# Delta rule: the first product of each doubling level from 32 by 32 blocks on array tiles of 32 by 32

## The chip, the cores and the metric

The kernel runs on one core of a Trainium2 chip, in one launch. The metric is the device time of that launch in microseconds (us); three runs of the kernel before the change gave 3674.04 (median), 3671.25 and 3676.92.

## The reference

Three layers run over one sequence of T = 2048 tokens with 1024 features, all in float32: sliding-window attention, a gated recurrence, and a hybrid layer whose two halves are a gated linear attention (GLA) and an RWKV-7 delta rule with 8 heads of 64. The change lies in the delta rule. Cut to what is computed there:

```python
def step(S, inp):                       # S: (head, value dim 64, key dim 64)
    r_t, w_t, k_t, v_t, kk_t, a_t = inp
    sa = einsum('bhvk,bhk->bhv', S, -kk_t)
    S = S * w_t[:, :, None, :] + sa[..., None] * (kk_t * a_t)[:, :, None, :] + v_t[..., None] * k_t[:, :, None, :]
    y = einsum('bhvk,bhk->bhv', S, r_t)
    return S, y
_, y = lax.scan(step, S0, xs)           # over 2048 tokens
```

The kernel doesn't scan token by token. It takes chunks of 64 tokens, in which the steps amount to a unit triangular system of 64 by 64 for each head. The inverse of that matrix is built by doubling: from the inverses of the diagonal blocks of size h (2, 4, 8, 16, 32) come those of size 2h, with the block under the diagonal being a product of three blocks: inverse, part of the matrix, inverse.

## The kernel before

`build` calls the phases one after the other; `delta_rule(k, h_saved)` comes after attention and the recurrence, and before the gated linear attention. Everything named below is in it.

**Tiling.** The 2048 tokens are 4 groups of G = 512, the 8 heads are 4 pairs p. That makes 16 units u = (group, pair), and each unit has two halves s of 256 tokens, so SN = 32 steps s. One step holds 4 chunks of 64 tokens for 2 heads: in SBUF the 128 partitions are two chunks c = 0, 1 (64 rows each), and the free dimension holds head h, chunk pair j and 64 columns. `m5(s)` is the part of the system matrix, `xz5(s)` the inverse so far and its transpose (index 0 and 1).

**A doubling level.** `halve(l, s, ...)` on TensorE (L2562 to L2585) does level l = 1 to 5 with h = 2^l, in two parts with a `yield` between them. The first part, L2564 to L2570, is called a here (l3a is that of level 3): for each h, j and c one product of the stored matrix with the inverse, 64 by 64 by 64, into one PSUM bank: 8 products. Its rows are `half(c)` and its output partitions `half(1 - c)`, so the 8 use two of the four array tiles of 64 by 64, the two off the diagonal. The second part, L2577 to L2584, is called b: VectorE (L2990) has multiplied a's result by the 0/1 mask `low{l}` into `t1`, and b multiplies the inverse with it from both sides: 8 products at L2580 (levels 1 to 4 alone) and 8 at L2583, all four tiles of 64 by 64 at levels below 5. VectorE adds them to the inverse at L2994 and L2995. `row // (2h) == small // (2h)` in the mask means that at levels 1 to 4 (2h up to 32) only the two diagonal blocks of 32 by 32 of a's result are used, and at level 5 only the block under the diagonal.

A product of float32 operands is two pairs of instructions, each pair a weight load and a matmul on the same array tile. So 8 products are 16 matmul records.

**The order of the work.** `in_turn` (L2436) writes the order of every engine's instructions by hand. It runs i over SN + 4 rounds of ten turns; in each turn TensorE takes one piece of `solve(i - 3)`, one of `scores(i - 2)`, one of `carry(i - 4)`, and then a number of pieces of `front(i)`. Front is the input projection: `product` (L194 to L196), three matmuls of 128x512 with 128 by 128 weights a piece. So each turn is a short section of small products between two stretches of front. The ten turns' sections on TensorE, before the change:

- turn 0: `lk` (L2626), l3a, transposes of `scores` (L2595), the first carry product c0 (L2674)
- turn 1: l3b, `m` and `x` (L2603, L2612), c1
- turn 2: l4a, c2
- turn 3: l4b, l1a, c3
- turn 4: l5a, l1b, `y` (L2681)
- turn 5: l5b, l2a, the mean over a head (L2687)
- turn 6: `wu` (L2638), l2b, the variance (L2691)
- turns 7 and 8: `gu` and `ry` of `solve`

The products c0 to c3 carry the state from chunk to chunk, 2 products (4 records) each on the two diagonal tiles of 64 by 64; c(i) waits for VectorE's update of the state (a `stt`, recorded at L183) after c(i-1). VectorE's pieces follow the same order in each turn: solve, scores, carry, front.

Of the kernel before, what the change touches and what calls it, by code (L numbers as in the profile page):

```python
# [2334 lines left out]
def delta_rule(k, h_saved):  # L2335
# [8 lines left out]
    def room(words):  # L2344

        if k.used + words <= k.arena_words:
# [30 lines left out]
    groups = [(g, p) for g in range(NG) for p in range(4)]  # L2377
    UN, SN = len(groups), 2 * len(groups)
    half = lambda i: slice(64 * i, 64 * i + 64)
    cols_of = lambda g: slice(g * G, (g + 1) * G)  # L2380
    lo_of = lambda g, c: k.hT_cut[:, c, cols_of(g)]
    hi_of = lambda g, c: k.hT_cut[:, c, cols_of(g // 2 if g == 2 else 0)] if g else k.oT_cut[:, 4 + c // 2, T // 2 + c % 2 * G:T // 2 + (c % 2 + 1) * G]
# [2 lines left out]
    m5 = lambda s: m_at[s % 2].rearrange("p (h i j m t) -> p h i j m t", h=2, i=2, j=2, m=2)  # L2385
    xz5 = lambda s: xz_at[s % 2].rearrange("p (m h j t) -> p m h j t", m=2, h=2, j=2)
# [8 lines left out]
    blocks = [("w", g, None) if p is None else (kind, g, p) for g in range(NG)  # L2395
              for p, kind in [(None, "w")] + [(p, kind) for p in range(4) for kind in "krvz"]]
# [96 lines left out]
    def on_pe():  # L2493
        mm = pe.matmul
        k.settle(pe)

        def bank(from_ring, kind, n):
            b, before = from_ring.take(kind, n)
            if before is not None:
                pe.wait_ge(*taken(*before))  # L2500
            return b
# [60 lines left out]
        def halve(l, s, ring, steps, came, t1, vec):  # L2562
            b = bank(ring, f"l{l}a", s)
            b4 = b[:, 0:SW].rearrange("p (h j t) -> p h j t", h=2, j=2)  # L2564
            pe.wait_ge(*came)
            for h in range(2):
                for j in range(2):
                    for c in range(2):
                        ins = mm(b4[half(1 - c), h, j, :], m5(s)[half(c), h, 0, j, 0, :], xz5(s)[half(c), 0, h, j, :], start=True, stop=True)
            ins.then_inc(*steps.did(f"l{l}a"))  # L2570
            yield
            x4 = bank(ring, f"l{l}X", s)[:, 0:SW].rearrange("p (h j t) -> p h j t", h=2, j=2) if l < 5 else None
            z4 = bank(ring, f"l{l}Z", s)[:, 0:SW].rearrange("p (h j t) -> p h j t", h=2, j=2)
            pe.wait_ge(*vec.by(f"t{l}", s))
            for h in range(2):
                for j in range(2):
                    if l < 5:  # L2577
                        for c in range(2):
                            o = half(1 - c)
                            mm(x4[half(c), h, j, :], xz5(s)[o, 1, h, j, :], t1[o, h, j, :], start=True, stop=True)  # L2580
                    for c in range(2):
                        o = half(1 - c)
                        ins = mm(z4[o, h, j, :], t1[o, h, j, :], xz5(s)[o, 1, h, j, :], start=True, stop=True)  # L2583
            ins.then_inc(*steps.did(f"l{l}b"))  # L2584
            yield  # L2585

        def scores(s):
# [26 lines left out]
            yield  # L2614
            yield
            yield from halve(1, s, sb, Spe, Sv.by("xd", s), t14[0], Sv)
            yield from halve(2, s, sb, Spe, Sv.by("X1", s), t14[0], Sv)

        def solve(s):
# [3 lines left out]
            for j in range(2):  # L2623
                for h in range(2):
                    for c in range(2):
                        ins = mm(b4[half(1 - c), j, h, :], m[half(c), h, 1, j, 0, :], tm[half(c), 2, j, h, :], start=True, stop=True)  # L2626
            ins.then_inc(*Vpe.did("lk"))
            yield from halve(3, s, sb, Vpe, Sv.by("X2", s), t14[1], Vv)
            yield from halve(4, s, sb, Vpe, Vv.by("X3", s), t14[1], Vv)
            yield from halve(5, s, sb, Vpe, Vv.by("X4", s), t14[1], Vv)  # L2630
# [459 lines left out]
def build(nc, ins, out, x1, x2, h2, spans, at):  # L3090
    with ExitStack() as ctx:
        k = Core(nc, ctx, ins, spans, at)
        constants(k)
        x0 = ins["x"][0]
        h_saved = h2.rearrange("(c p) t -> p c t", p=P)
        attention(k)
        finish_layer(k, x0, x1, ins["attn_w_out"][0], ins["attn_b_out"][0], ins["post_norm_w"][0], "pre1", None, head=RecurrenceHead)
        recurrence(k)
        finish_layer(k, x1, x2, ins["rec_w_out"][0], None, ins["post_norm_w"][1], "norm2", None, h_saved)
        delta_rule(k, h_saved)  # L3100
        gla(k)
        finish_layer(k, x2, out, ins["w_out_2"][0], None, None, None, ins["final_norm_w_2"])
        for s in k.stores:
            k.sp.wait_ge(*s.end())
# [32 lines left out]
```

## Time and profile before

| | |
|---|---|
| median of 3 runs (lowest, highest) | 3674.04 us (3671.25, 3676.92) |
| the profiled execution | 3675.65 us, its span 3674.4 us |
| granted TensorE clock, mean | 0.984 |
| PE (TensorE matmul) busy | 3497.8 us, 95% |
| PEld (weight load) busy | 2820.5 us, 77% |
| DVE (VectorE) busy | 2057.0 us, 56% |
| ACT (ScalarE) busy | 1719.8 us, 47% |
| POOL (GpSimd) busy | 1346.6 us, 37% |

PE busy is the union of the matmul records' spans. Their ends are modelled and overlap the next records by far (a record of 64 columns lasts 218 ns), so the time that a group of matmuls takes is read from the starts, not from the durations: the last start of a group is its start plus the group's time less the duration of one record.

### The profile page before, as it was taken

What the parts mean: (1) busy time and instruction counts of PE and PEld (TensorE: products, weight loads), DVE (VectorE), ACT (ScalarE), POOL (GpSimd) and SP (SyncE); (2) the same over time, 40 slices, a digit from 0 to 9 for tenths busy, and PEclk for the clock granted to TensorE, in tenths of its full rate; (3) what the DMA queues carried; (4) which work ended last, traced back from release to release, by engine and by line L of the source; (5) the groups of instructions that cost most, each with busy time, mean ns of one, the idle gap of its engine ahead of it and who ended that gap; (6) DMA issues with size and microseconds to landing.
All of it is one profiled execution on the core that took longest, in us unless ns stands there. A gap on an engine that the chain in (4) does not pass through costs nothing. (4 is left out here: it accounts for less than half of the span.)

```text
span 3674.4 us, 83152 instructions
## 1 busy us (share of the span) xinstructions
PE 3497.8 (95%) x34784; PEld 2820.5 (77%) x34784; DVE 2057.0 (56%) x4664; ACT 1719.8 (47%) x3161; POOL 1346.6 (37%) x1681
## 2 busy tenths in 40 slices
PE   8999998899899999999998989999999997999999
PEld 7888785688788877888787867777777776788777
DVE  4566766755655657555555446666666665343422
ACT  3455555522555556555554344444444442444522
POOL 5333321132444554544543323222232220544332
PEclk9999999999999999999998999999999998999999
DMA  4322211232110111101112341111111113322322
GB/s 137 92 66 78 61 53 35 81 104 93 30 41 24 41 30 30 41 24 41 30 35 86 135 138 48 43 43 41 44 37 43 43 37 111 86 70 70 104 81 92
DMA packets 252243, 231.26 MB, mean 63 GB/s; under 512 B 9120, under 2 KB 223072, under 8 KB 251872
## 3 DMA queue, kind: packets, MB, share of 16 engines
q1 hardware_dynamic: 251872, 225.94, 20.2%
q8 instruction: 279, 4.57, 0.5%
q14 instruction: 92, 0.75, 0.1%
HBM read 192.35 MB, written 33.55 MB: 61 GB/s over the span
## 5 line engine op out<-in xcount | busy, mean ns | idle before, releaser
L195 PE MATMUL bank<-hT_cut,arena_cut 128*128 128x512 f32 x2048 | 803.8, 392 | 0.0
L188 ACT ACTIVATE arena<-bank 128x512 f32<-128x512 f32 (+1 forms) x584 | 315.9, 570 | 585.0 <-PE bank L196 295.3
L194 PE MATMUL bank<-hT_cut,arena_cut 128*128 128x512 f32 x1240 | 552.4, 445 | 0.0
L196 PE MATMUL bank<-hT_cut,arena_cut 128*128 128x512 f32 x1240 | 488.1, 394 | 0.0
L194 PE MATMUL bank<-arena_cut,hT_cut 128*128 128x512 f32 (+1 forms) x1280 | 458.2, 358 | 27.0 <-DVE arena_cut L1152 22.4
L188 ACT ACTIVATE arena<-arena 128x512 f32<-128x512 f32 (+3 forms) x674 | 350.0, 555 | 251.3 <-POOL arena L1600 191.8
L195 PE MATMUL bank<-arena_cut,hT_cut 128*128 128x512 f32 (+1 forms) x1280 | 448.5, 350 | 0.0
L195 PEld LDWEIGHTS bank<-hT_cut,arena_cut 128*128 128x128 f32 x2048 | 387.3, 189 | 78.5 <-issue 18.6
L189 ACT ACTIVATE arena<-arena 128x256 f32<-128x256 f32 (+2 forms) x336 | 210.3, 627 | 411.4 <-DVE arena L178 187.5
L2850 POOL TENSOR_TENSOR arena_cut<-arena,arena_cut 128x256 fp32r<-128x256 f32 x272 | 218.1, 833 | 409.0 <-ACT arena_cut L188 409.0
L715 POOL TENSOR_TENSOR arena_cut<-arena,arena_cut 128x256 fp32r<-128x256 f32 x288 | 216.2, 779 | 412.9 <-ACT arena_cut L188 412.8
L194 PE MATMUL bank<-oT_cut,arena_cut 128*128 128x512 f32 x808 | 349.5, 433 | 7.1 <-POOL arena_cut L2850 5.1
L188 ACT ACTIVATE arena_cut<-arena 128x1024 fp32r<-128x1024 f32 (+2 forms) x338 | 294.8, 888 | 53.6 <-DMA arena<-in_attn_w_in 34.7
L196 PE MATMUL bank<-oT_cut,arena_cut 128*128 128x512 f32 x808 | 318.9, 395 | 0.0
L196 PE MATMUL bank<-arena_cut,oT_cut 128*128 128x512 f32 x768 | 305.5, 398 | 0.0
L1591 POOL TENSOR_TENSOR arena_cut<-arena,arena_cut 128x256 fp32r<-128x256 f32 x248 | 197.5, 820 | 286.2 <-ACT arena_cut L188 286.2
L194 PEld LDWEIGHTS bank<-arena_cut,hT_cut 128*128 128x128 f32 x1280 | 242.2, 189 | 74.5 <-issue 31.9
L194 PEld LDWEIGHTS bank<-hT_cut,arena_cut 128*128 128x128 f32 x1240 | 233.0, 188 | 71.9 <-issue 22.0
L196 PEld LDWEIGHTS bank<-hT_cut,arena_cut 128*128 128x128 f32 x1240 | 232.8, 188 | 53.5
L195 PEld LDWEIGHTS bank<-arena_cut,hT_cut 128*128 128x128 f32 x1280 | 242.3, 189 | 35.4 <-issue 1.4
L196 PE MATMUL bank<-arena_cut,hT_cut 128*128 128x256 f32 x896 | 250.4, 280 | 0.0
L188 ACT ACTIVATE arena<-bank,arena 128x512 f32<-128x512 f32 (+1 forms) x176 | 90.0, 559 | 291.3 <-PE bank L196 260.5
(269 smaller groups left out, 7194.3 us busy)
## 6 DMA issues: line engine op xcount, KB each, us to landing
arena<-in_w_in SPq DMA_DIRECT2D x100, 512.0 KB, 3.8
arena<-in_attn_w_in SPq DMA_DIRECT2D x144, 256.0 KB, 2.8
arena<-in_rec_w_in SPq DMA_DIRECT2D x62, 512.0 KB, 4.1
x_after<-arena SPq DMA_DIRECT2D x32, 512.0 KB, 2.6
arena<-x_after SPq DMA_DIRECT2D x32, 512.0 KB, 4.1
arena<-in_x SPq DMA_DIRECT2D x16, 512.0 KB, 3.6
h_after<-hT SPq DMA_DIRECT2D x4, 2048.0 KB, 7.7
hT<-h_after SPq DMA_DIRECT2D x4, 2048.0 KB, 16.5
```

The source lines that it names most:

```text
L188: return e.activation(out, a, f, bias=bias, scale=scale)
L189: return e.activation(out, a, f, bias=bias, scale=scale, accum_out=accum)
L194: pe.matmul(out, a[0], b[0], start=start, stop=False)
L195: pe.matmul(out, a[0], b[1], start=False, stop=False)
L196: return pe.matmul(out, a[1], b[0], start=False, stop=stop)
L715: ins = pool.tensor_tensor(w_lo[n % WN][:, c, :], raw[n % WN][:, c, :], w_hi[n % WN][:, c, :], ALU.subtract)
L1591: ins = pool.tensor_tensor(w_lo[i][:, c, :], raw[i][:, c, :], w_hi[i][:, c, :], ALU.subtract)
L2850: ins = pool.tensor_tensor(w_lo[n % 3][:, c:c + 2, :], raw[n % 3][:, c:c + 2, :], w_hi[n % 3][:, c:c + 2, :], ALU.subtract)
```

## The change

The product a is cut into blocks of 32 by 32. At levels 1 to 4 each of the 8 products becomes two, for the two diagonal blocks (`blocks` = (0,0), (1,1)); at level 5 it becomes one, for the block under the diagonal ((0,1): rows 0 to 31 of the operands, output partitions of the lower half). Rows and outputs are at `quarter(...)`, so each product runs on an array tile of 32 by 32 with 32 moving columns. What of the bank isn't written any more is what the mask multiplies by zero. Nothing else changes: not the bank, the wait, the semaphore increment after the last product, the mask, nor the order of the turns.

```diff
+    quarter = lambda i: slice(32 * i, 32 * i + 32)
...
             b4 = b[:, 0:SW].rearrange("p (h j t) -> p h j t", h=2, j=2)
             pe.wait_ge(*came)
+            blocks = [(r, r) for r in range(2)] if l < 5 else [(0, 1)]
             for h in range(2):
                 for j in range(2):
-                    for c in range(2):
-                        ins = mm(b4[half(1 - c), h, j, :], m5(s)[half(c), h, 0, j, 0, :], xz5(s)[half(c), 0, h, j, :], start=True, stop=True)
+                    for r, to in blocks:
+                        for c in range(2):
+                            rows, own = quarter(2 * c + r), quarter(2 * (1 - c) + to)
+                            ins = mm(b4[own, h, j, quarter(r)], m5(s)[rows, h, 0, j, 0, quarter(to)], xz5(s)[rows, 0, h, j, quarter(r)],
+                                     start=True, stop=True)
             ins.then_inc(*steps.did(f"l{l}a"))
```

## Rows read from the trace of the kernel before

**Rows 1.** The page: the span, and TensorE's busy time, share and instructions.
```profile
span 3674.4 us, 83152 instructions
PE 3497.8 (95%) x34784; PEld 2820.5 (77%) x34784; DVE 2057.0 (56%) x4664; ACT 1719.8 (47%) x3161; POOL 1346.6 (37%) x1681
```

**Rows 2.** Windows: the stage of the delta rule.
```profile
2222.60:3106.60 884.00, 860.25 (x16537) 662.90 (x16538) 574.03 (x1362) 386.62 (x771) 241.28 (x274) 0.99 0.18 50
```

**Rows 3.** Groups by form: count, busy us, mean ns; then idle before.
```profile
L2569 PE MATMUL bank<-oT 64*64 64x64 f32 x2560 | 107.5, 224 | 2.3 <-DVE oT L2994 1.2 <-issue 0.9 <-DVE oT L3004 0.2
L2580 PE MATMUL bank<-oT 64*64 64x64 f32 x2048 | 85.2, 223 | 3.2 <-DVE oT L2990 3.1
```

**Rows 4.** Timeline of TensorE, a turn 2: start us, us, what.
```profile
2667.51 0.39 PE L195 MATMUL bank<-hT_cut,arena_cut 128*128 128x512 f32 x1
2667.74 0.40 PE L196 MATMUL bank<-hT_cut,arena_cut 128*128 128x512 f32 x1
2668.06 0.68 PE L2569 MATMUL bank<-oT 64*64 64x64 f32 x16
2668.66 0.33 PE L2674 MATMUL bank<-arena,oT 64*64 64x64 f32 x4
2668.92 0.51 PE L194 MATMUL bank<-hT_cut,arena_cut 128*128 128x512 f32 x1
```

**Rows 5.** Timeline of VectorE over the same turn.
```profile
2667.72 0.69 DVE L3013 TENSOR_TENSOR oT<-oT,arena 128x512 f32<-128x512 f32 x1
2668.32 0.28 DVE L183 SCALAR_TENSOR_TENSOR arena<-bank,arena,oT 128x64 f32<-128x64 f32 x1
```

**Rows 6.** Timeline of TensorE, the head of a turn 0.
```profile
2660.11 0.68 PE L2626 MATMUL bank<-arena,oT 64*64 64x64 f32 x16
2660.62 0.63 PE L2569 MATMUL bank<-oT 64*64 64x64 f32 x16
2661.19 1.09 PE L2595 MATMUL bank<-common_table,arena 128*128 128x128 f32 x8
```

**Rows 7.** Timeline of TensorE, a turn 3.
```profile
2670.52 0.27 PE L2580 MATMUL bank<-oT 64*64 64x64 f32 x2
2670.53 0.27 PE L2583 MATMUL bank<-oT 64*64 64x64 f32 x2
...
2671.03 0.46 PE L2569 MATMUL bank<-oT 64*64 64x64 f32 x10
2671.29 0.27 PE L2674 MATMUL bank<-arena,oT 64*64 64x64 f32 x2
...
2671.44 0.22 PE L2569 MATMUL bank<-oT 64*64 64x64 f32 x2
2671.60 0.50 PE L194 MATMUL bank<-hT_cut,arena_cut 128*128 128x512 f32 x1
```

**Rows 8.** Timeline of TensorE, a turn 4.
```profile
2672.49 0.62 PE L2569 MATMUL bank<-oT 64*64 64x64 f32 x14
2672.91 0.27 PE L2583 MATMUL bank<-oT 64*64 64x64 f32 x2
...
2673.99 0.50 PE L194 MATMUL bank<-hT_cut,arena_cut 128*128 128x512 f32 x1
```

**Rows 9.** Timeline of TensorE, a turn 5.
```profile
2648.63 0.51 PE L2583 MATMUL bank<-oT 64*64 64x64 f32 x10
2648.92 0.27 PE L2569 MATMUL bank<-oT 64*64 64x64 f32 x2
...
2649.53 0.70 PE L2687 MATMUL bank<-oT,common_table 128*128 128x256 f32 x2
```

**Rows 10.** Lines L2569 and L1932: weight loads of 64 and 32 columns, ns min/median/max.
```profile
L2569 PEld LDWEIGHTS bank<-oT x2560: 129/135/227, 2222.6 to 3103.3; 64*64 64x64 f32 x197
L1932 PEld LDWEIGHTS bank<-hT,arena x64: 106/110/178, 3126.1 to 3370.5; 128*32 128x32 f32 x64
```

**Rows 11.** Timeline of TensorE in the recurrence: two tiles of 64 columns, 32 moving columns.
```profile
1500.36 0.66 PE L1410 MATMUL bank<-arena 128*64 128x32 f32 x16 [0.80 <-DVE arena L1691]
```

## The prediction

> **What bounds the kernel now.** I read the page first: TensorE is busy for 95% of the span and no other engine for more than 56% [rows 1]. Then the window of the delta rule, the only stage that the change touches: 884 us long, TensorE busy for 860 of them, VectorE for 574 [rows 2]. So time on TensorE in this stage counts almost fully, in either direction, and the question is what the groups at L2569 cost it. The busy time of that line is 107.5 us for 2560 records, 3.4 us for each of the 32 steps s [rows 3]. This is no price, since records overlap by most of their 0.22 us; only starts tell. So I went to the timeline and read one turn of each kind in which the line stands. Turns of one kind repeat to 0.01 us, and the gaps to front around them are at their least (0.32 us before), so TensorE doesn't wait there.
>
> **How the array is paced now.** Three terms come out of these turns.
> - A tile's own turn. In turn 0, `lk` and l3a use the same two tiles, and l3a starts 0.51 us after `lk` [rows 6]. Of that 0.05 is the first weight load, which nothing hides; the other 0.46 to 0.47 are 8 turns of two records side by side, 0.058 each. With four tiles the turn is the same, and 32 records take the same 0.51 (b to a in turn 3) [rows 7]. So it is the tile that paces and not the record: with 16 records on two tiles a costs 0.47, a record each 29 ns; with four tiles a record comes each 15 ns.
> - A change of the tile's shape. From the last matmul of front to the first of a there are 0.32 us, against 0.23 between two of front [rows 4]: 0.09 more. From a's last start to the first transpose in turn 0 there are 0.15 (l3a starts 0.63 - 0.22 = 0.41 to 0.42 after its first, at 2661.04) [rows 6], of which 0.058 are the last record's own turn: again 0.09. In addition the first weight load of the new shape lies open.
> - Overlap without such a change. In turn 3, c3 runs on the two diagonal tiles while l1a is still on the other two: it starts at 2671.29, l1a's last record at 2671.44, and front follows 0.16 later [rows 7]. c3 costs nothing. In turn 5, l2a starts 0.29 after l5b, while l5b goes on to 0.46 [rows 9]: 0.17 are shared.
>
> **What the change does to a group a.** It makes 32 records of the 16 at levels 1 to 4, on four tiles of 32 by 32; at level 5 it keeps 16, on two such tiles. A tile's turn should fall with the 32 columns of both operands. A weight load of 32 columns is 23 ns shorter than one of 64 (106 against 129) [rows 10], and streaming 32 columns in place of 64 must not bind. That the weights bind is seen where a tile has 64 weight columns but only 32 moving ones: 16 records on two tiles still take 0.66 us, as here [rows 11]. 58 less 23 is 35 ns, and half of 58 would be 29; I take 32, between them. Bounds: 0.026 (four tiles whose records start 7 ns apart, the first two pairs of b: four starts in 0.02 us [rows 7]) and 0.058 (no shorter than now). So at 0.032 a four-tile group takes 0.025 + 7 x 0.032 + 0.02 = 0.265 from its first start to its last; at level 5, 0.25.
>
> But each group now stands between two changes of shape, from 64 to 32 and back, and shares nothing with its neighbours. A change after 64 columns costs 0.15 from last start to first start, after 32 columns 0.09 + 0.03 = 0.12; I take the 0.09 of rows 4 and 6 for these pairs too. Bounds: 0 (a tile of 32 that lies inside one of 64 is no change for the array) and the 0.09.
>
> The page "TensorEngine Tiling (Array Packing)" of the Trainium skill says in its section on key properties that going from one tiling mode to another, not merely from one tile to another, drains the engine. Rows 4 and 6 show such a drain between 128 and 64; between 64 and 32 nothing here shows it, and the page says it of any two modes. By the page the sum is the one below; were only tiles with 128 rows meant, it would be the rival without a drain.
>
> **Turn by turn**, from a turn's first start to the next front (or the next fixed point), now and after:
> - Turn 0 (`lk`, l3a, transposes): the transposes start at 0.51 + 0.57 = 1.08 [rows 6]. After: `lk` 0.46, change 0.15, l3a 0.265, change 0.12: 1.00. That is -0.08.
> - Turn 2 (l4a, c2): l4a would be over at 0.27 and c2 could start at 0.39, but c2 starts at 0.60 now although l4a's last record started at 0.46 [rows 4]: it waits for VectorE's state update, which runs from 2668.32 to 2668.60 behind a mask at L3013 [rows 5]. That chain begins in turn 1, which the change leaves as it is. In other turns 2, c2 comes as late as 0.8. So 0.
> - Turn 3 (l4b, l1a, c3): now 1.08 [rows 7]. After: b's last start 0.48, change 0.15, l1a 0.265, change 0.12, c3 in the open 0.11 (c2's 0.33 less a record's 0.22 [rows 4]), change to front 0.15: 1.27. That is +0.19.
> - Turn 4 (l5a, l1b, y): l1b starts at 0.42 and front at 1.50 [rows 8]. After: l1b at 0.25 + 0.12 = 0.37, then 0.48 (b) + 0.42 (y) + 0.15: 1.42. That is -0.08.
> - Turn 5 (l5b, l2a, mean): the mean's product starts at 0.90 [rows 9]. After: 0.46 + 0.15 + 0.265 + 0.12 = 1.00. That is +0.09.
> - Turns 1, 6, 7 and 8 hold no group a: 0.
>
> The sum of a step is +0.12 us, for 32 steps +3.9. At the ends of the stage groups stand alone: the first step of `scores` has no l4b and l5b beside it (turns 3 and 5 are then 0.46 + 0.15 less 0.265 + 0.12, so 0.23 shorter each, rather than 0.19 and 0.09 longer), and the second has no c3. Together that is -1.0. Net +2.9 us. The profiled execution took 3675.65 (span 3674.4 and 1.25 around it), so it would take 3678.5; it lies 1.6 above the median of the three runs, and against that median I forecast 3677.
>
> VectorE gets a's result up to 0.2 us earlier after its turn began, but its mask product is only needed in the next turn, with front between: TensorE waited 3.1 us of the whole stage for it at L2580 [rows 3], and that is all there is to win. The stage's 2048 more records (of 34784 [rows 1]) cost what the groups cost; no other engine gets an instruction more. Front hides nothing here: it is TensorE's own work and moves with the rest.
>
> **The rivals.**
> - B, slower: the records come no faster than now. The fastest steady pace that the trace shows is 15 ns a record, four tiles at 64 columns [rows 7], and there the tile paced it. If TensorE's supply of instructions has its limit near that, 32 records take 0.45 and not 0.265. That is +0.19 in turns 0, 3 and 5; turn 2 still ends before c2's wait, and level 5 with two tiles doesn't need the pace. 3 x 0.19 x 32 = +18 us: 3695. For it: no row shows 8 ns a record over more than four. Against it: four start within 0.02. It decides from about 10 ns a record, where four tiles ask for more than a turn of 0.032 gives. "TensorE: Matmul & The Clock Gate" of the Trainium skill (back-to-back issue gap) has an issue floor of about 25 ns for a small moving operand; here records 15 ns apart contradict it as a limit over several tiles, so it takes nothing from the sum, but it makes a floor somewhat likelier.
> - C, faster: between 64 and 32 nothing drains. Then a group gives back 0.47 - 0.25 = 0.21 in turns 0, 3 and 4, and 0.04 to 0.21 in turn 5, by how much is still shared; some 0.75 us a step, -24 us: 3650. Against it: every change of shape that I found cost the same 0.09, those between 64 and 128 in both directions among them [rows 4, 6].
> - D, much slower: the four row tiles of a group write into one PSUM bank, and take turns at it. 32 records at 0.032 one after the other are 1.02 us: +0.76 in turns 0, 3 and 5, +0.26 in turn 4, and about +0.45 in turn 2, where c2 would have to wait: 3.0 x 32 = +96: 3773. Against it: the two row tiles of today's a write one bank at full pace [rows 6]. The same tiling page, in its restrictions, says that different row tiles cannot access one PSUM bank at the same time; the trace differs for two.
>
> **How the numbers follow.** My sum (A) 0.50, its own range 3672 to 3683: the tile turn between 0.026 and 0.040 moves 7 intervals in four turns, -5 to +7 us at most, less in turn 4 and with the runs' own scatter of 3. B 0.26, C 0.15, D 0.03, and 0.06 for mixtures, most of them slower. The range of 3664 to 3702 holds A, B and some of the rest; C and D are left out. A difference under 0.2% (7.3 us) can't be told from none here. Faster by more than that: C and a little of A, 0.16. Within: A less its edges, 0.46. Slower: B, D, the upper edge of A and the mixtures, 0.38.
>
> **What would show it.** In the profile after, a turn 0 has L2569's successor in about 0.48 us as the timeline has it (0.265 and a record's duration), 0.15 after `lk`, the transposes 0.12 after it. Turn 3 shows c3 behind l1a and 1.27 us in all; turns 4 and 5 show 1.42 and 1.00. B is seen by 32 records in 0.65 and more; C by an `lk` and an l3a with 0.06 or less between them; D by 1.2. In turn 2, c2 must stay at 0.60 to 0.80 after l4a's start: if it comes earlier, the wait was not VectorE's, and up to 0.2 us a step is gained that I gave away. The forecast is wrong if TensorE's time in the stage moves by more than 7 us either way.

## The result, and the profile after

| | before | changed |
|---|---|---|
| median of 7 runs (lowest, highest) | 3674.04 us (3671.25, 3680.25) | 3684.10 us (3677.31, 3689.98) |
| ratio, 95% interval | | 1.0022 [1.0012, 1.0033] |
| the profiled execution, its span | 3675.65, 3674.4 us | 3684.10, 3682.8 us |
| granted TensorE clock of the profiled execution | 0.984 | 0.983 |
| mean granted clock of the 7 runs | not recorded | 0.9817 |

The changed kernel is slower: by the ratio about 8 us, by the medians 10, in the profiled pair 8.4. That is small, but clear of the scatter. Its page shows the 2048 additional records and a busy time that has not grown, against [rows 1]:

```profile
span 3682.8 us, 87248 instructions
PE 3496.9 (95%) x36832; PEld 2813.6 (76%) x36832; DVE 2056.9 (56%) x4664; ACT 1719.1 (47%) x3161; POOL 1345.8 (37%) x1681
```

By form, the line of group a (L2573 now, L2569 before; every line behind it is 5 higher) has 4608 records in 73.7 us, where 2560 had 107.5 [rows 3]. The groups b after it have 115.1 (L2588; 113.2 before) and 87.7 (L2585; 85.2 before [rows 3]), since less of them is shared:

```profile
L2588 PE MATMUL bank<-oT 64*64 64x64 f32 x2560 | 115.1, 229 | 1.6 <-issue 1.6
L2585 PE MATMUL bank<-oT 64*64 64x64 f32 x2048 | 87.7, 226 | 2.8 <-DVE oT L2995 2.7
L2573 PE MATMUL bank<-oT 32*32 32x32 f32 x4608 | 73.7, 195 | 5.1 <-issue 3.8 <-DVE oT L2999 0.9 <-DVE oT L3009 0.2
```

Busy time on such a page would have called this a gain of 34 us. The starts show why it is none. Timelines of TensorE (start us, us, what), a turn 0, against [rows 6]:

```profile
2662.49 0.68 PE L2631 MATMUL bank<-arena,oT 64*64 64x64 f32 x16
2663.10 0.45 PE L2573 MATMUL bank<-oT 32*32 32x32 f32 x32
2663.48 1.09 PE L2600 MATMUL bank<-common_table,arena 128*128 128x128 f32 x8
```

l3a starts 0.61 behind `lk` (0.51 before) and the transposes 0.38 behind l3a (0.57 before): 0.99 and not 1.08. A turn 2, against [rows 4], and the end of a turn 3 whose first record started at 2672.80, against [rows 7]:

```profile
2670.34 0.45 PE L2573 MATMUL bank<-oT 32*32 32x32 f32 x32
2670.94 0.33 PE L2679 MATMUL bank<-arena,oT 64*64 64x64 f32 x4
2671.20 0.51 PE L194 MATMUL bank<-hT_cut,arena_cut 128*128 128x512 f32 x1
...
2673.42 0.45 PE L2573 MATMUL bank<-oT 32*32 32x32 f32 x32
2673.81 0.33 PE L2679 MATMUL bank<-arena,oT 64*64 64x64 f32 x4
2674.07 0.50 PE L194 MATMUL bank<-hT_cut,arena_cut 128*128 128x512 f32 x1
```

In turn 2, l4a is through 0.2 us earlier and c2 still starts 0.60 after l4a's start: nothing won. It waits for the same state update on VectorE as before [rows 5], which ends 0.05 us ahead of it:

```profile
2670.61 0.28 DVE L183 SCALAR_TENSOR_TENSOR arena<-bank,arena,oT 128x64 f32<-128x64 f32 x1
```

In turn 3, c3 stands behind l1a, in the open, and the turn takes 1.27 us instead of 1.08. A turn 4, against [rows 8], and a turn 5, against [rows 9]:

```profile
2674.97 0.44 PE L2573 MATMUL bank<-oT 32*32 32x32 f32 x16
2675.34 0.27 PE L2585 MATMUL bank<-oT 64*64 64x64 f32 x2
...
2675.80 0.23 PE L2588 MATMUL bank<-oT 64*64 64x64 f32 x2
2675.86 0.63 PE L2686 MATMUL bank<-oT,arena 64*64 64x64 f32 x16
2676.43 0.50 PE L194 MATMUL bank<-hT_cut,arena_cut 128*128 128x512 f32 x1
...
2650.91 0.68 PE L2588 MATMUL bank<-oT 64*64 64x64 f32 x16
2651.52 0.45 PE L2573 MATMUL bank<-oT 32*32 32x32 f32 x32
2651.91 0.70 PE L2692 MATMUL bank<-oT,common_table 128*128 128x256 f32 x2
```

Turn 4 takes 1.46 (1.50 before), and the mean's product of turn 5 starts at 1.00 (0.90 before). These are no lucky picks: over the steady steps turn 3 is 0.192 us longer on the mean, turn 5 0.09 longer and turn 4 0.034 shorter, and none of them varies by more than 0.01 from step to step (turn 5 within each of its forms, with and without other products).

Where in the stage the 8 us lie is read from windows that end at the same piece of work: from a's first record to the transposes of step 28, and from there to the last y (columns: window, its length, busy time of PE, PEld, DVE, ACT, POOL, then granted clock, DMA share, GB/s). Before:

```profile
2222.60:2999.05 776.45, 767.05 (x14416) 588.26 (x14415) 508.29 (x1191) 353.96 (x701) 228.56 (x260) 1.00 0.16 42
2999.05:3114.40 115.35, 97.99 (x2253) 78.14 (x2250) 69.75 (x184) 35.01 (x77) 12.71 (x14) 0.93 0.29 98
```

After:

```profile
2222.90:3003.32 780.42, 765.68 (x16191) 580.15 (x16191) 507.40 (x1191) 353.60 (x701) 228.38 (x260) 1.00 0.16 42
3003.32:3122.90 119.58, 100.03 (x2531) 79.12 (x2524) 69.84 (x184) 35.07 (x77) 12.69 (x14) 0.91 0.29 95
```

4.0 us come in 28 steps at the full clock, and 4.2 more in the last 115 to 120 us. In the first 54 us of these front still runs, and there the two kernels differ by 0.4 us; the other 3.8 come after front's last matmul. From there on the last steps' small products follow one another with waits between them, and the granted clock has stretches at its low level (0.5 of full, so 1.2 of 2.4 GHz): 15.8 us of them before, 21.1 in the changed kernel, worked out from the clock in the traces. The steady part has a cleaner measure in which the first steps don't count, 26 steps from the transposes of step 2 to those of step 28: 738.57 us before, 743.01 after, +0.171 a step. The experiments take these two parts separately.

### The profile page after: what moved, and what is told of

The parts are those of the page before. It is cut to its first block and busy times, and to the rows that moved or that the text cites. A ratio compares the mean times of both kernels' runs of the same rounds, so it can differ in the third digit from the quotient of the medians.

```text
span 3682.8 us, 87248 instructions
## 1 busy us (share of the span) xinstructions
PE 3496.9 (95%) x36832; PEld 2813.6 (76%) x36832; DVE 2056.9 (56%) x4664; ACT 1719.1 (47%) x3161; POOL 1345.8 (37%) x1681
```

## The experiments

Theory T is the prediction's: a change of tile shape costs 0.09 us and an open weight load, and nothing is shared across it. Rival R: the time goes with the number of records. Each kernel is the changed one with the edit shown, but for held_before, which is the kernel before with it.

**1. Which levels: l35 and l12.** The edit, in `halve`, with (3, 5) and (1, 2):

```diff
                 for j in range(2):
+                    if not (l in (3, 5)):
+                        for c in range(2):
+                            ins = mm(b4[half(1 - c), h, j, :], m5(s)[half(c), h, 0, j, 0, :], xz5(s)[half(c), 0, h, j, :], start=True, stop=True)
+                        continue
                     for r, to in blocks:
```

> Blocks of 32 by 32 at levels 3 and 5 alone; levels 1, 2 and 4 stay on tiles of 64. Theory T (the change of tile shape costs 0.09 us and the open weight load, and takes away the sharing of the array): turn 0 shorter by 0.08 us, turn 4 by 0.03, turns 3 and 5 as before the change (1.08 and 0.90 to the mean); 32 x -0.11 = -3.6 us in the steady part, so 3670 to 3671 where before is 3674. Rival R (the time goes with the number of records, 8 us over 2048 more of them, 4 ns each): 512 more records, +2 us.

> Blocks of 32 by 32 at levels 1 and 2 alone. Theory T: turn 3 longer by 0.19 us and turn 5 by 0.09, all others as before; 31 x 0.28 less 0.7 at the first steps = +8 us, the whole of the changed kernel's loss and a little more. Rival R (4 ns for each additional record): 1024 more records, +4 us.

Measured: l35 0.9988 [0.9980, 0.9997], median 3671.54, against 3676.55 for the kernel before measured beside it. l12 1.0030 [1.0017, 1.0042], 3687.31. The 26 steady steps took 736.05 us in l35, 2.5 less than before, and 745.57 in l12, 7.0 more. The two differences add up to +4.5, and the changed kernel has +4.4. R has both slower; T has the sign of each and, at -0.097 and +0.269 us a step against -0.11 and +0.28, the size. The same change is a gain at two levels and a loss at two others. Over the whole launch l12 lost 10.8 us where T had 8; 4.7 of them lie in the end of the stage (120.0 us from step 28 to the last y, 115.4 before), which is taken up in experiment 4.

**2. Same records, one change of shape fewer: swap3.**

```diff
-    def in_turn(cut, solve, scores, carry, front):
+    def in_turn(cut, solve, scores, carry, front, first=()):
...
-                for gen in late:
+                for gen in ([late[1], late[0], late[2]] if n in first else late):
...
-        in_turn(nothing, solve, scores, carry, front)
+        in_turn(nothing, solve, scores, carry, front, first=(3,))      # TensorE's alone
```

> The changed kernel, with TensorE taking l1a ahead of l4b in turn 3, so that the turn has one change of tile shape fewer (128, 32, 64, 128 instead of 128, 64, 32, 64, 128). Theory T: 0.26 (l1a) + 0.12 (change) + 0.48 (l4b) + 0.06 + 0.11 (c3) + 0.15 = 1.18 us instead of 1.27 for the turn; 31 x -0.09 = -2.8 us against the changed kernel, with the same records. Rival R (the records cost the time): no difference.

The timeline of its turn 3:

```profile
2612.09 0.45 PE L2573 MATMUL bank<-oT 32*32 32x32 f32 x32
2612.47 0.27 PE L2585 MATMUL bank<-oT 64*64 64x64 f32 x2
...
2613.00 0.28 PE L2679 MATMUL bank<-arena,oT 64*64 64x64 f32 x4
2613.21 0.51 PE L194 MATMUL bank<-hT_cut,arena_cut 128*128 128x512 f32 x1
```

1.12 us for the turn with the same 68 records that took 1.27: shorter than the 1.18 expected, since c3 now follows products of its own shape: its four records start within 0.06 us (0.28 less 0.22) and not the 0.11 that they take behind a change. The steady steps took 739.38 us, 3.6 less than in the changed kernel. R is refuted here, with the records held fixed. Over the whole launch the gain can't be told from none: the ratio to the kernel before is 1.0016 [1.0007, 1.0026], median 3681.92, where the changed kernel has 1.0022 [1.0012, 1.0033]. In the profiled execution the end of the stage took the gain back (123.1 us from step 28 to the last y, 119.5 in the changed kernel), with 38 us at the low clock in it.

**3. Group b in the small shape too: b4in32.** At level 4 alone:

```diff
+                    if l == 4:
+                        for r in range(2):
+                            q = quarter(r)
+                            for c in range(2):
+                                o, i = quarter(2 * (1 - c) + r), quarter(2 * c + r)
+                                mm(x4[i, h, j, q], xz5(s)[o, 1, h, j, q], t1[o, h, j, q], start=True, stop=True)
+                            ...
+                        continue
...
+            if l == 4:
+                for m, kind in enumerate("XZ"):
+                    for i in range(4):
+                        part = xz[quarter(i), m, :, quarter(i % 2)]
+                        ins = v.tensor_tensor(part, part, four(kind)[quarter(i), :, quarter(i % 2)], ALU.add)
```

> The changed kernel, with l4b too from blocks of 32 by 32: 32 products (64 records) on eight tiles instead of 16 on four, and VectorE adding only the diagonal blocks at this level, in 8 operations instead of 2. Nothing changes shape between l4b and l1a. Theory T with the tile as the pace: l4b 0.29, l1a 0.26, change 0.12, c3 0.11, change 0.15: 0.93 us for turn 3 instead of 1.27. If records can't come faster than one each 7 ns, l4b takes 0.45 and the turn 1.10. Both are -5 to -10 us against the changed kernel, less what VectorE's additional operations delay. Rival R: 1024 more records, +4 us.

Measured: 1.0148 [1.0131, 1.0165], 3729.66 us, far worse than either expected. TensorE's turn 3 and the start of turn 4, then VectorE in the same stretch:

```profile
2665.55 0.22 PE L2587 MATMUL bank<-oT 32*32 32x32 f32 x2
...
2666.10 0.21 PE L2590 MATMUL bank<-oT 32*32 32x32 f32 x2
2666.16 0.45 PE L2573 MATMUL bank<-oT 32*32 32x32 f32 x32
2666.54 0.33 PE L2689 MATMUL bank<-arena,oT 64*64 64x64 f32 x4
2666.80 0.50 PE L194 MATMUL bank<-hT_cut,arena_cut 128*128 128x512 f32 x1
...
2667.69 0.44 PE L2573 MATMUL bank<-oT 32*32 32x32 f32 x16
2669.34 0.27 PE L2595 MATMUL bank<-oT 64*64 64x64 f32 x2 [1.21 <-DVE oT L3005]
```

```profile
2666.36 2.38 DVE L3012 TENSOR_TENSOR oT<-oT,bank 32x128 f32<-32x128 f32 x8
2668.77 0.42 DVE L3005 TENSOR_TENSOR oT<-bank,arena 128x256 f32<-128x256 f32 x1
```

The part of it that T was asked about: between l4b and l1a there are only 0.06 us, so nothing like the 0.12 us of a change of shape, as T says of groups of one shape. But l4b's 64 records took 0.61 us to l1a's start and not 0.29, so the turn is 1.25 long: 9.5 ns a record over eight tiles is the pace here, and no longer the tile, whose 8 records would need 8 x 0.032 us. What sets this pace (the supply of instructions, or the writes into the two banks) no run tells apart. The loss is VectorE's: eight additions of 32 partitions take 2.38 us where two of 128 take 0.8, and l1b, which needs the mask product queued behind them, waits 1.2 us. The steady steps took 776.38 us, 33 more than in the changed kernel.

**4. The end of the stage: steady, tail, and the loads held.** The condition of experiment 1 with s < 28 and s >= 28.

> Blocks of 32 by 32 at all levels, but only in steps s below 28; the last four steps run on tiles of 64. In the traces the changed kernel is 4.4 us behind at s = 28 and 8.4 behind at the end of the stage. If the second 4 us come from the changed groups in the last steps (U1), this kernel is 4.4 us behind at s = 28 and still 4 to 5 behind at the end. If they come from where the clock's low stretches and the instruction fetches fall in the sparse end of the stage, and so from chance (U2), its last part may take anything from that of before to 4 us more, and differ from run to run.

> The converse: blocks of 32 by 32 only in the steps s from 28 on. U1: equal to before up to s = 28, then +4 us: 3678. U2: equal up to s = 28, then what the four steps' turns give by theory T, 4 x 0.16 = +0.6 us, plus or minus up to 4 us that differ from run to run.

The steady steps came out as expected: 742.90 and 738.63 us. Over all: steady 1.0012 [1.0003, 1.0021], median 3680.95; tail 1.0004 [0.9996, 1.0013], 3678.00. From step 28's transposes to the last y the profiled executions took 116.3 and 116.4 us, between 115.4 (before) and 119.5 (changed), which decides nothing between U1 and U2, since one such stretch differs from the next. (U1 had tail 4 us over the kernel before; it is 1.4 over by the medians, and its interval reaches from -1.5 to +4.8 us.) In it TensorE waits for nothing that the profile shows ("issue") for 6.1 us before, 7.2 after, 3.1 in l35 and 8.5 in l12, longest 4.6 us at once, and this hides what the change does. The next edit is to take these waits away:

```diff
         sp.wait_ge(*Fpe.by("z", UN - 1))
+        sp.wait_ge(*Cv.by("out", SN - 1))
         for g in range(NG):
             sp.wait_ge(*moved[g])
```

> The kernel before, with the four loads that bring the hidden state back into SBUF held until the last step's output is written. This makes the start of the GLA stage late by some 15 us; what is looked at is the end of the delta rule alone, from the transposes of step 28 to the y of the last step (115.4 us before, 119.5 in the changed kernel), in which TensorE is idle for 6.1 and 7.2 us on nothing that the profile shows. If these are instruction fetches that the big loads hold up, the idle time falls to under 2 us and the stretch to 110. If not, both stay.

> The same edit on the changed kernel. If the loads cause the idle time, the stretch falls to the same 110 us plus 0.6 for four steps. If the additional 4 us of the changed kernel there come from something else, it stays 4 us longer than in the kernel before with the same edit.

The same stretch, kernel before with the edit:

```profile
3001.60:3111.10 109.50, 94.35 (x2250) 75.88 (x2250) 69.52 (x184) 35.03 (x77) 12.70 (x14) 0.97 0.05 13
```

and changed kernel with the edit:

```profile
3005.80:3119.50 113.70, 99.06 (x2537) 78.61 (x2525) 69.58 (x184) 35.12 (x77) 12.69 (x14) 0.91 0.05 12
```

The issue waits are gone in both, so they came of the loads that the edit holds: the four of 2 MB and the two of 512 KB behind them in the same queue. That they are waits for instructions is not shown. The kernel before gains about 6 us here (115.4 to 109.5), but this isn't their price alone: waits for VectorE grew (that of `lk` from 1.7 to 4.6 us), and the time at the low clock fell from 15.8 to 6.8.

The 4 us between the two kernels stay, so the issue waits don't explain them. TensorE is not idle for longer either (15.2 us without, 14.6 with small tiles). What differs is the clock: 0.97 of full against 0.91, or 6.8 us at the low level after front's end against 21.0. The record shows that the 4 us are lost there. Take the mean over a head, `wu` and the variance in turns 5 and 6 near the end, groups that no edit touches and that follow each other without a wait. Kernel before with the edit, the timeline and the window:

```profile
3102.72 0.70 PE L2688 MATMUL bank<-oT,common_table 128*128 128x256 f32 x2
3103.40 1.09 PE L2639 MATMUL bank<-oT 64*64 64x128 f32 x16
3104.48 0.67 PE L2692 MATMUL bank<-oT,common_table 128*128 128x256 f32 x2
3102.72:3104.48 1.76, 1.76 (x21) 1.21 (x19) 0.85 (x2) 0.42 (x1) 0.00 (x0) 1.00 0.03 9
```

Changed kernel with the edit:

```profile
3109.71 1.22 PE L2693 MATMUL bank<-oT,common_table 128*128 128x256 f32 x2
3110.86 1.97 PE L2644 MATMUL bank<-oT 64*64 64x128 f32 x16
3112.76 0.70 PE L2697 MATMUL bank<-oT,common_table 128*128 128x256 f32 x2
3109.71:3112.76 3.05, 3.05 (x20) 2.07 (x18) 0.84 (x2) 0.42 (x1) 0.00 (x0) 0.50 0.02 5
```

From the mean's first start to the variance's it takes 1.76 us at the full clock and 3.05 at the low one, for the same work. Cut the whole stretch of the two traces into pieces of 1.5 us and more at the starts of such groups: the pieces that ran at the full clock in both kernels differ by 0.3 us in all, and those that had the low clock in one of them or in both by 3.8. A second pair, with four runs each:

> The kernel before with the four loads held, again, for the clocks of many runs. In one look each, the stretch from the transposes of step 28 to the last y had 6.8 us at the low clock in this kernel and 20.5 in the changed one, without any idle time for the instruction fetch in either. Theory C: its mean granted clock is higher than that of the changed kernel with the same edit, by 0.002 or more. Rival (where the low stretches fall is chance): the two means lie within their errors of each other.

> The changed kernel with the four loads held. Theory C: mean granted clock lower by 0.002 or more than with the same edit on the kernel before, and 4.3 us (the turns) plus 2 us for each 0.001 of clock longer, so 8 to 9. Rival: 4.3 us longer, at the same clock.

Mean clock of the four runs of each 0.9808 and 0.9785, standard errors 0.0006 and 0.0003; medians 3695.91 and 3708.87. The clock is lower by 0.0023, as C expects, but the kernel is 13 us slower by the medians and 11 by the ratios, more than its 8 to 9. Of the 14.8 us between the two profiled executions 6.8 lie ahead of the first group a, where the kernels do the same, so chance has a part in it; the end of the stage has 3.9 (6.8 us at the low clock against 17.1 after front's end), the steady steps 4.4. Cut into the same pieces, the stretch differs by 1.3 us where both ran at the full clock, 0.8 of it in a single piece, and by 2.6 in the rest.

Across the kernels, the mean clocks of all runs, with the standard error:

| kernel | runs | clock | small tiles in the last four steps |
|---|---|---|---|
| before, beside experiments 1 to 4 | 41 | 0.9833 (0.0002) | none |
| before, beside experiment 5 | 15 | 0.9830 (0.0003) | none |
| best (experiment 5) | 11 | 0.9845 (0.0003) | none |
| steady | 11 | 0.9828 (0.0004) | none |
| l12 | 6 | 0.9828 (0.0003) | levels 1, 2 |
| l35 | 11 | 0.9827 (0.0006) | levels 3, 5 |
| changed | 7 | 0.9817 (0.0004) | all levels |
| tail | 11 | 0.9816 (0.0003) | all levels |
| swap3 | 10 | 0.9813 (0.0003) | all levels |
| b4in32 | 4 | 0.9793 (0.0005) | all levels, and group b of level 4 |

Within the 41 runs of the kernel before, the time goes with the clock at 2.0 us for each 0.001 (a straight line through them; correlation -0.84). By that line, which is an estimate, the changed kernel's 0.0016 are worth 3 us, and at equal clock it is 5 slower than before; `tail` at equal clock is not slower than before at all. In the profiled pair the changed kernel has only 5.3 us more at the low clock, half of what the runs have on the mean.

So much is shown: the extra time of the held pair's end is spent at the low clock, and kernels with small tiles at all levels in the last four steps had a lower mean clock over their runs, `tail` by 0.0017, over four standard errors. That the small tiles are what brings it down is not shown. The profile of `tail` has 16.6 us at the low clock after front's end, no more than that of `steady` (16.8), and `best`, without a small tile there, lies 0.0015 above the kernel before measured beside it, nearly as far as `tail` lies below. How the work falls in time may do as much as the shape of the tiles. Why the clock falls is open too: every low stretch between the first step and the last y comes after front's last matmul in the kernel before and in the changed one, where TensorE has idle time, but the held pair shows no more idle time with the small tiles.

**5. What the others point to: best.** The condition of experiment 1 with `l in (3, 5) and s < 28`.

> Blocks of 32 by 32 at levels 3 and 5 alone, and only in steps below 28: the two levels whose turns got shorter, and tiles of 64 throughout the sparse end of the stage. Theory T: turn 0 shorter by 0.083 us and turn 4 by 0.034, 28 x -0.117 = -3.3 us in the steady part (l35 showed -2.5 over 26 steps). Theory C (the small tiles of the last steps lower the granted clock): the mean clock is that of the kernel before, 0.9833, where the kernel with levels 3 and 5 in all steps had 0.9827. So 3 to 5 us under before. Rival: the difference between these clocks is chance, and this kernel and l35 are the same.

Measured: 0.9978 [0.9969, 0.9987], median 3668.67 against 3676.37 for the kernel before beside it, steady steps 736.53 us (2.0 less than before), mean clock 0.9845 (0.0003) over 11 runs. It beats both kernels, the changed one by about 0.4%. That is 8 us under before, where 3 to 5 were expected, and the turns of the steady steps account for only 2 of them. Against l35 it gains in the end of the stage (111.7 us from step 28 to the last y, 115.1 in l35) and in clock; the difference of the two clocks, 0.9845 and 0.9827, is 2.7 of their standard error, more than chance would mostly give, though the mean of `best` lies above the kernel before's as well, which nothing here explains and Theory C does not foresee.

## Why the prediction was right, and where it was off

I forecast 3677, no difference that can be told, with 0.38 for slower; it is 3684.10 and 0.22% slower, just over the 0.2% that I counted as none, and inside the range. The range is no proof of the sum: it reaches to 3702 for rival B, which did not come, and the sum's own range ended at 3683. The sign that I had named for a wrong forecast, 7 us in TensorE's stage, was met: the stage is 8.2 us longer (891.8 to 900.0 by the windows above). The mechanism of the turns was right, and half of the loss was in no term. By its steps:

- A tile's turn with 32 columns, 0.032: right. 32 records took 0.45 - 0.19 = 0.26 us in every turn (0.265 forecast), 16 at level 5 0.25 (0.25 forecast).
- The change of shape between 64 and 32, 0.15 and 0.12: right, on nothing but rows for 64 and 128. `lk` to l3a 0.61 - 0.46, l3a to the transposes 0.38 - 0.26. The rule of "TensorEngine Tiling (Array Packing)" in the Trainium skill, section Key Properties, that any change of mode drains the engine is what the trace shows here too; swap3 and b4in32 show that groups of one mode go on without that gap. Rival C is out.
- Turn 0 -0.08, turn 2 none (c2 waits for VectorE), turn 3 +0.19, turn 5 +0.09: each as forecast, to 0.01.
- Turn 4: -0.03, forecast -0.08. The step that was off is "then 0.48 (b) + 0.42 (y)": y's first start is 0.06 behind b's last (2675.86 against 2675.80 above), so that it comes 0.52 and not 0.48 behind b's first. It was 0.52 before the change too (from 2672.91 [rows 8] to 2673.43), a row that the prediction didn't show. 32 x 0.05 is 1.6 us.

```profile
2673.42 0.23 PE L2580 MATMUL bank<-oT 64*64 64x64 f32 x2
2673.43 0.63 PE L2681 MATMUL bank<-oT,arena 64*64 64x64 f32 x16
```

- Rival B: 32 records weren't held back, and B is out for this change. b4in32 shows that 64 over eight tiles come no faster than 9.5 ns each, whatever holds them.
- Rival D: four row tiles, each with output partitions of its own, wrote one bank, 32 records in 0.26 us. "TensorEngine Tiling (Array Packing)" in the Trainium skill says under Gotcha 1 that row tiles can't access one bank at the same time; the pace of this trace shows nothing of it.
- The end of the stage: "Net +2.9" took it for more of the same at the full clock. After front's last matmul, from level 3 of step 29 on, the changed kernel has more time at the low clock: about 3 us on the mean of the runs by the estimate above. That term was missing from the sum, which put it at nothing; neither it nor a rival named the clock, though the row of the stage had 0.99 in it [rows 2] and its last 115 us 0.93. What brings the clock down stays open.

So what the runs have in place of +2.9 is +4.4 in the 26 steady steps (of which 1.2 is turn 4's term), less at the first steps, a little in the last four, plus some 3 of clock.

## What to carry to other kernels

Read what a small product costs from the starts in its neighbourhood, not from its busy time: here the busy time of the line fell by 34 us and the kernel got slower, because the group lost what it shared with its neighbours on the other tiles and gained a change of shape on each side. Change the tile shape where a change is due anyway (before a stretch of 128 by 128, or after one), and leave it where groups of one shape follow one another; the same edit was worth -0.1 us a step at two levels and +0.27 at two others. Look at the sparse end of a stage by itself, with the granted clock beside it: half of this kernel's loss lies there, and its cause is not settled.

## What the runs showed of the hardware that was not expected

- In b4in32 the first 32 of 64 records of l4b start within about 0.16 us, 5 ns each, and the other 32 come 9 to 10 ns apart; all 64 start in 0.55 us. With 32 records on four tiles (8.2 ns each) no such slowing is seen.
- Four loads of 2 MB (and two of 512 KB behind them) beside the dense small products of the stage's end went with 6.1 us (before) and 7.2 us (changed kernel) in which TensorE waits for nothing that the profile shows; holding the loads removed them. (Here holding them costs more than it brings, since the next stage starts later.)
- An addition on VectorE over 32 partitions takes 0.30 us (2.38 for 8) and one over 128 partitions with twice the columns 0.41: cut into eight, the work of two additions took three times as long.
- The same two groups (mean and `wu`) took 1.76 us at the full clock and 3.05 at the low one.
